# Linear mixer's states grown without a mask, weights placed between the halves of the bias, mixing issued ahead of the waiting turnings

## The reference, cut to what matters

```
# differential attention, head h, tokens i >= j
s1, s2 = q1 k1^T + bias, q2 k2^T + bias
o_h    = (softmax(s1) - lam * softmax(s2)) v_h

# gated linear attention, chunk n of 64 tokens, head h
o_n[h]     = (q_dec[h] k_inv[h]^T * causal) v[h]  +  q_dec[h] state_n[h]
state_n+1[h] = decay_n * state_n[h] + k_end[h]^T v[h]      # state: 32 keys x 64 values

mixed = concat(o, gla, pool);  h = h + mixed w_out
```

## Time and profile before

| | us |
|---|---|
| median of 3 runs (2662.98 to 2666.08) | 2665.7 |
| profiled execution, its own time | 2665.57 |
| profiled execution, span | 2663.8 |
| the stage of the mixers in the span, about | 2059 to 2187 |

### The profile page before, as it was taken

The page is one execution under the profiler, slowest core; times in us unless marked ns, Lnnn a source line. Parts: engine busy times, 40 slices in busy tenths (PEclk is TensorE's granted clock), DMA queues, the critical chain, the costliest instruction groups (busy, mean ns, idle before and its releaser), DMA issues. The chain is left out here.

```text
span 2663.8 us, 53388 instructions
## 1 busy us (share of the span) xinstructions
PE 2468.5 (93%) x23961; PEld 1817.7 (68%) x23961; DVE 1125.5 (42%) x2089; ACT 408.9 (15%) x955; POOL 221.5 (8%) x209
## 2 busy tenths in 40 slices
PE   7999989799999998999899798888889979999999
PEld 3586655587787774588787555444458757888888
DVE  4662654511111115446675332323254465335542
ACT  2112540300000002100231100000011441110000
POOL 0000000122222210000001100000010301000000
PEclk9999999899999999999999899999989989999999
DMA  8351316699999994114555999999942101222311
GB/s 320 134 184 60 123 74 237 260 360 405 408 407 407 405 406 187 63 48 124 158 169 218 362 422 421 423 422 423 422 157 103 64 1 64 91 84 80 118 74 45
DMA packets 89852, 594.94 MB, mean 223 GB/s; under 512 B 10880, under 2 KB 34368, under 8 KB 44392
## 3 DMA queue, kind: packets, MB, share of 16 engines
q1 hardware_dynamic: 74888, 558.54, 52.9%
q0 software_dynamic: 12000, 22.48, 3.3%
q10 hardware_dynamic: 2736, 10.49, 1.0%
HBM read 574.33 MB, written 16.10 MB: 222 GB/s over the span
## 5 line engine op out<-in xcount | busy, mean ns | idle before, releaser
L1287 PE MATMUL moe_ps<-room,moe_xs 128*32 128x256 f32 x9616 | 554.1, 382 | 53.8 <-DMA room<-in_experts 38.9
L1287 PEld LDWEIGHTS moe_ps<-room,moe_xs 128*32 128x32 f32 x9616 | 388.0, 111 | 217.6 <-issue 62.0
L1287 PE MATMUL moe_ps<-room,moe_hid_t 128*32 128x256 f32 x4640 | 263.9, 381 | 12.2 <-DMA room<-in_experts 9.3
L1287 PEld LDWEIGHTS moe_ps<-room,moe_hid_t 128*32 128x32 f32 x4640 | 184.9, 110 | 90.4 <-issue 14.3
L1620 DVE TENSOR_TENSOR moe_hid<-moe_silu,moe_ps 128x512 f32<-128x512 f32 x32 | 22.0, 687 | 314.3 <-PE moe_ps L1287 254.2
L1549 DVE SCALAR_TENSOR_TENSOR x_feat<-moe_ps,mod,x_feat 128x512 f32<-128x512 f32 (+1 forms) x144 | 95.9, 730 | 126.7 <-PE moe_ps L1349 115.0
L1492 ACT ACTIVATE moe_silu<-moe_ps 128x512 f32<-128x512 f32 x32 | 19.1, 597 | 757.9 <-PE moe_ps L1287 723.9
L1640 DVE TENSOR_SCALAR moe_y<-moe_ps,moe_gates 128x256 f32<-128x256 f32 x42 | 17.7, 478 | 255.1 <-PE moe_ps L1287 255.1
L1330 POOL DMA_INDIRECT acc<-moe_y,moe_sum_ids x42 | 69.1, 1644 | 331.3 <-DVE moe_y L1640 322.8
L2079 PE MATMUL mlstm_psg<-h_feat,room 128*128 128x384 f32 x256 | 90.4, 497 | 1.3 <-ACT room L2175 1.3
L1850 PE MATMUL v_ps<-room,h_feat 128*128 128x256 f32 x384 | 86.0, 382 | 0.0
(11 more groups left out here) (725 smaller groups left out, 3805.0 us busy)
## 6 DMA issues: line engine op xcount, KB each, us to landing
room<-in_experts SPq DMA_DIRECT2D x144, 2048.0 KB, 36.6
room<-in_experts SPq DMA_DIRECT2D x67, 1024.0 KB, 13.0
moe_slot<-in_experts SPq DMA_DIRECT2D x22, 1024.0 KB
feed_f_slots<-in_ffn_gate SPq DMA_DIRECT2D x11, 1024.0 KB, 4.9
feed_f_slots<-in_ffn_up SPq DMA_DIRECT2D x11, 1024.0 KB, 4.8
feed_f_slots<-in_ffn_down SPq DMA_DIRECT2D x8, 1408.0 KB, 6.1
room<-in_ada_w SPq DMA_DIRECT2D x10, 1024.0 KB, 5.5
qk_ada_w<-in_ada_w SPq DMA_DIRECT2D x8, 1024.0 KB, 5.3
```

What stands on the lines that cost most here:

```text
L1287: mm = pe.matmul(group_ps(part, g)[32 * q:32 * q + 32], turned[:, k * GROUP:(k + 1) * GROUP], weights[:, m, q], start=(k == 0 and g != 1), ...
```

## The change

All edits are in `hybrid_tables` and `hybrid_mixers`:

```diff
 # tables: "heads" is neither allocated nor loaded; 10 tables are awaited instead of 11
-                    pe.wait_ge(sig["combined"], u + 1)
                     if u >= 1:
                         pe.wait_ge(sig["turned_out"], u)
+                    if u in (6, 12, 13, 14):
+                        keep_awake(pe, K, ps[:, 6], 3)
+                    pe.wait_ge(sig["combined"], u + 1)
                     for j in range(i + 1):                       # turn(u)
...
-                    pe.wait_ge(sig["grown"], N - 1 + t)
+                    pe.wait_ge(sig["grown"], N - 1 - t)           # pool_product(t)
...
-                    pe.wait_ge(sig["states"], 1)
+                    pe.wait_ge(sig["grown"], N - 1)               # linear_mix(pair)
                     to = ps[:, (pair + 1) % 2]
                     for t in range(LT):
-                        for n in (2 * t, 2 * t + 1):
-                            pe.matmul(to[:, n * C:(n + 1) * C], state(n)[:, pair * P:(pair + 1) * P],
-                                      q_dec[:, n * C:(n + 1) * C], start=(n % 2 == 0), stop=False, skip_group_check=True)
                         for h in (2 * pair, 2 * pair + 1):
-                            rows = slice(GLA_DV * (h % 2), GLA_DV * (h % 2 + 1))
+                            rows, keys = slice(GLA_DV * (h % 2), GLA_DV * (h % 2 + 1)), slice(GLA_DK * h, GLA_DK * (h + 1))
+                            for n in (2 * t, 2 * t + 1):
+                                pe.matmul(to[rows, n * C:(n + 1) * C], state(n)[keys, h * GLA_DV:(h + 1) * GLA_DV],
+                                          q_dec[keys, n * C:(n + 1) * C], start=(n % 2 == 0), stop=False, skip_group_check=True)
...
-                    elif u == 10:                                 # PE loop
-                        outer(7)
...
+                    if u >= 2:
+                        mix(u - 2)
                     if 1 <= u <= NUM:
                         turn(u - 1)
...
-                    if u >= 2:
-                        mix(u - 2)
...
                 def grow(n):
                     dve.wait_ge(sig["outer"], n + 1)
-                    dve.tensor_tensor(grown[:, n % 2], ps[:, (n + 1) % 2, 0:W], T["heads"][:], ALU.mult).then_inc(sig["grown"], 1)
-                    if n + 1 < N:
-                        dve.wait_ge(sig["grown"], n + 1)
-                        step(dve.scalar_tensor_tensor(state(n + 1), state(n), decay[:, n:n + 1], grown[:, n % 2],
-                                                      ALU.mult, ALU.add))
+                    if n:
+                        dve.wait_ge(sig["grown"], n)
+                    dve.scalar_tensor_tensor(state(n + 1), state(n), decay[:, n:n + 1], ps[:, (n + 1) % 2, 0:W],
+                                             ALU.mult, ALU.add).then_inc(sig["grown"], 1)
...
                     for m in range(2):                            # DVE loop
+                        if m and u >= 1:
+                            weights(u - 1)
                         dve.wait_ge(sig["scores"], 2 * u + m + 1)
                         dve.scalar_tensor_tensor(s[:, u % 3, m, 0:n], ...)
-                    if u >= 1:
-                        weights(u - 1)
...
-                    elif u == 10:
-                        grow(7)
-                        dve.sem_inc(sig["states"], 1)
```

More of the change, by code:

```diff
@@ L2866, in hybrid_tables @@
     T = {"w_lr": sb("w_lr", [P, KT, 32]), "gla_gate_w": sb("gate_w", [P, P]), "keep": sb("keep", [P, LAT]),
-         "causal": sb("causal", [P, P]), "heads": sb("heads", [P, GLA_HEADS * GLA_DV]), "reverse": sb("reverse", [P, P]),
+         "causal": sb("causal", [P, P]), "reverse": sb("reverse", [P, P]),
          "spread": sb("spread", [P, 4, 32]), "back": sb("back", [P, 3, P]), "rel_bias": sb("rel", [32, DA_HEADS])}
@@ L2874, in load @@
     def load(pool, sig):
-        for n in ("w_lr", "bucket", "rel_bias", "never", "gla_gate_w", "spread", "back", "reverse", "keep", "causal", "heads"):
+        for n in ("w_lr", "bucket", "rel_bias", "never", "gla_gate_w", "spread", "back", "reverse", "keep", "causal"):
             dst = T[n] if n in ("bucket", "never") else T[n][:]
@@ L2883, in load @@
                            ).then_inc(sig["pool_w"], 16)
-    T["load"], T["count"] = load, 11 * 16
+    T["load"], T["count"] = load, 10 * 16
     return T
@@ L2913, in hybrid_mixers @@
         q_dec, k_inv, k_end = ya, yc, yd
-        k_tok, grown = z[:].rearrange("p (t c) -> p t c", c=P), low[:].rearrange("p (r w) -> p r w", w=W)
+        k_tok = z[:].rearrange("p (t c) -> p t c", c=P)
         last_root = z
@@ L3587, in constants @@
     out["causal"] = ((p[:, None] <= p[None, :]) & (p[:, None] // 64 == p[None, :] // 64)).astype(f)
-    out["heads"] = (p[:, None] // GLA_DK == np.arange(256)[None, :] // GLA_DV).astype(f)
     r, upper = p % 32, (p >= 64).astype(int)
```

## The result

The changed kernel takes 2671.69 us (median of 12 runs), the kernel before 2665.53 (12 runs). The ratio is 1.0021, interval 1.0012 to 1.0029: 5.6 us slower, between 3.2 and 7.7 (the two medians lie 6.2 apart; the ratio is used from here on). The forecast was 2660.9, range 2657.0 to 2666.6, so the measured time lies outside the range. The execution that was profiled is a short one, 2666.93 us with a span of 2665.2, but its first 2055 us, which the change doesn't touch, were 3.9 us shorter than in the profile of before. So the stage is compared by itself, from its first product to the first of the next stage. First row: before; last two: after.

The account below looks back on a forecast made before the run. TensorE, busy in 93% of the span, was taken as the bound, with time won where it idles or is slow. Terms +0.2 - 6.4 + 0.2 + 1.4 + 0.3 - 0.4 = -4.7 from 2665.57 gave 2660.9 us, range 2657.0 to 2666.6.

Parts of the forecast that it names:

- A: Up to turning 6: mixing issued ahead of turning 4, largely absorbed by one masking product less and DVE slack; +0.2 us.
- B: Turning 6 to 9: clock stays up, DVE's waits for outer products go, state updates get cheaper; -6.4 us.
- C: Turning 9 to the linear mixing: outer and masking products go, two waits for exponentials come; +0.2 us.
- D: The two linear mixings: narrow state products at 0.0925 us a record, +1.4 us, and the order, +0.3 us.
- The order: Around the linear mixings: mix(9) leaves the way between them and mix(10) comes in ahead of turning 11; +0.3 us.
- The pace at 2.4 GHz: In the two linear mixings: all records at 0.0925 us, 4.44 us a mixing; +0.7 us each, +1.4 in all.
- E: Behind turning 12: mix(11) fills part of a wait, so ACT's 0.30 us goes, 0.1 more ahead of turning 13; -0.4 us.
- The rival built on that rule: Linear mixings: 16 further changes between 32 and 128 rows drain the array, 2.2 us, total 2663.1; chance 0.13.
- the term it adds to: The two linear mixings' narrow records at 0.0925 us each: +0.7 us a mixing, +1.4 in all.
- The rival in which the clock falls in the mixing: Linear mixings and what follows run at 1.2 GHz, +4 to +5.6 us, about 2670.5; chance 0.07.
- The rival of overlapping narrow products: Linear mixings: the two heads' state products run at once, 3.0 us a mixing instead of 4.44, total 2658.0; chance 0.12.

Follow-up runs that it names:

- e3: The changed kernel with its narrow products reordered so that the two heads' scores' products stand next to each other; ratio 0.9990 to the kernel before.
- e7: e3 with state products on all 128 rows, still 64 columns wide (linear attention's output not the reference's); ratio 0.9962 to the kernel before.
- e12: The changed kernel, order kept, with state products on all 128 rows instead of 32 (linear attention's output not the reference's); ratio 0.9963 to the kernel before.
- e5: e3 with more idle products: three ahead of turning 5 and eight, not three, ahead of turning 6; ratio 0.9984 to the kernel before.
- e8: The kernel before with the new order, weights between the bias halves and idle products; masks and wide linear mixing kept; ratio 0.9984 to the kernel before.
- e2: The kernel before with the narrow linear mixing alone; masks, order and weights as before; ratio 1.0038 to the kernel before.
- e6_hold_mixing: e3 with one full-array idle product ahead of each of the eight blocks of the two linear mixings; ratio 1.0000 to the kernel before.
- e1: The changed kernel with the wide linear mixing of before, states unmasked (linear attention's output not the reference's); ratio 0.9987 to the kernel before.
- e9: e8 with state products of each head on 128 rows and 64 columns, in the order of e3, masks kept; ratio 0.9977 to the kernel before.
- e4: The changed kernel without its twelve idle products; ratio 1.0030 to the kernel before.
- e11: The changed kernel with q_dec masked per head by GpSimd, state products on 128 rows and 64 columns in the order of e3; ratio 0.9965 to the kernel before.
- e13: e11 with three idle products ahead of turning 5 and eight ahead of turning 6; ratio 0.9968 to the kernel before.

## Why the prediction was wrong, step by step

Milestones on PE, before and after (rows above), each from its stage's start:

- *A*, to turning 6: 75.98 and 76.37, +0.4; forecast +0.2.
- *B*, turning 6 to 9: 16.13 and 11.13, -5.0; forecast -6.4, which is 9.7 us left. The step's condition, that the clock holds, failed: it fell at about 2128.4, ahead of the idle products, and DVE still waited 1.14 us for an outer product of the slow PE, where it had waited 3.68. That this profile shows 11.13 is partly chance: the code up to the mixing is the same in e3, e7 and e12, and in their profiles the clock is low for some 3.5 us only, from about 77 us into the stage, and B takes 9.65 to 9.70. With the clock up throughout it is 9.58 (e5, 2137.34 to 2146.92). So the size was right, and the clock was not held by the idle products of the change. A state update takes 0.48 us busy in one instruction (seven of them, 3.3 us), within the bounds.
- *C*: 3.96 and 4.08, +0.1; forecast +0.2.
- *D*, mixing to turning 12: 12.95 and 23.60, **+10.65; forecast +1.7**. This is the step that failed. It has three parts. The order, forecast +0.3, is about +0.1: D is 12.95 before and 13.02 in e8, which has the new order with the wide mixing. The pace at 2.4 GHz: 2 x (5.87 - 3.73) = +4.3, where +1.4 was forecast. The rest, +6.3, is the clock, for which the sum had nothing: the two mixings together last 16.4 us instead of 2 x 5.9, and what stands behind them is slow as well.
- *E*: 20.06 and 19.41, -0.65; forecast -0.4.

Sum of the measured: +5.5, the stage's own difference.

What was mis-sized in D is the scores' record. I priced all 96 records at 0.0925. That held for the 64 state records, four of them 0.37. But 0.0925 was no price of a scores' product by itself. In the kernel before, the products of two heads stood side by side in the two column halves, so that a pair had the time of one, and four records shared what a group costs. I broke up that pair in the sum without asking. Alone, two to a group, they take 0.18. The rows could have warned: records of 128 columns at 0.0925 stand beside a mixing record of the same columns at 0.135.

The runs put another cause in the place of the order. With the order of the change kept, 128 rows instead of 32 give 2.13 us (e12): the column halves do overlap across states and scores, if all have one form. With 32 beside 128 they do not (changed kernel, e2), and each group costs some 0.13 us beside its records (the estimate at e3). The Trainium skill ("TensorEngine Tiling (Array Packing)", section "Key Properties") states that changing the tiling mode drains the array. The trace agrees, 5.9 against 2.1 us for one index. My argument against it in D misread its row. The eight 32-row records take 1.09 us between neighbours of other forms, and so do the eight mixing records compared with them, 1.08. Eight mixing records that follow transposes of their own form take 0.98 in the same trace, so a change is in both of the times that I held against each other:

```profile
2169.05 1.06 PE L2995 MATMUL hym_ps<-hym_wt,hy_v 128*128 128x128 f32 x8
2170.03 0.49 PE L2975 MATMUL hym_ps<-hy_f 64*128 64x128 f32 x4
```

The rival built on that rule priced a change at 0.135, near the estimate of 0.13, and came to 2.2 us in all, 3.6 with the term it adds to, against 4.3 measured. The rival in which the clock falls in the mixing came true as well, and was given 0.07. Both together were no rival of mine: each had been set against the same forecast, as if they excluded each other. The rival of overlapping narrow products stays untested: no run puts 32-row products of two heads next to each other.

Why the clock falls is open. In all seven profiles with 32-row state products it falls inside the mixings or right behind the first; in all nine with 128-row ones it stands at 1.00. In the changed kernel TensorE was busy without a gap ahead of the fall, and full-array idle products between did not prevent it (e6_hold_mixing). That the 32-row products bring it is shown by e12; what in them does, the rows themselves or the longer and thinner mixing that they make, is not.

The masks' part is less clear in the times than in the profiles. e8 (masks) and e1 (none) are level, 0.9984 and 0.9987; e9 and e7, with the fast mixing, differ by 0.0015, 4 us, with intervals that overlap. In the profiles the mixing starts 95.2 and 95.3 us into the stage with masks (e8, e9) and at 90.0 to 90.2 in e3, e4, e5, e7, e11, e12 and e13 without; 1.6 of these 5 us lie in C, where the clock fell a second time in e8 and e9 (90.8 to 94.2). Part of what is won is given back behind turning 12, where the later low clock begins sooner: E is 22.4 us in e7 (low from 111 to 128) and 19.3 in e9 (low from 121.5 to 128).

## What to carry to other kernels

Cutting products down to the rows that matter saved nothing here, and it cost: a product of 32 rows beside one of 128 ran alone, at some 0.13 us for each change between the two, while products of 128 rows in different column halves ran at once. Rather mask the moving operand, on an idle engine, and keep all products of a stretch in one form; where forms must differ, group them (e3 against the changed kernel: 8.3 us by the order alone). When a record is faster in the trace than its size allows, ask what stands next to it before its price is moved to another order.

## What the runs showed of the hardware that was not expected

- 64-column products on all rows, alternating between the column halves, ran at 2.13 us for 48 records, 0.044 us each, at 2.4 GHz; the same work with the whole width took 3.73 us for 32 records.
- Each group of products of one form cost some 0.13 us beside its records (an estimate from groups of four and eight records, 0.37 and 0.61 us, in e3).
- The clock fell with TensorE 100% busy (2148 to 2152: 4.00 of 4.00 us), among 32-row products.
- Three idle products ahead of turning 6 did nothing for the first fall: it begins at 77.2 us with them (e3) and at 77.0 without (e4), 3.5 us long in both. With three ahead of turning 5 and eight ahead of turning 6 the clock held (e5, e13).
